# High half first: the streamed weight blocks' sixteen products with the weights' high half ahead of the eight with the low half, each group behind its own wait

## The reference

```python
h = rms_norm(x, norm_g[l]);  proj = h @ w_in[l]            # 1024 x 6728, l = 0, 1
mkv = rms_norm(mem, mem_norm_g[l]) @ w_mem_kv[l]           # 1024 x 1024
merged = g0 * (y_pool @ w_branch[l, 0]) + g1 * (y_attn @ w_branch[l, 1]) + g2 * (y_mem @ w_branch[l, 2])
x = x + merged @ w_out[l]
# second block, 272 tokens
proj = h @ w_in_2                                          # q, k, v, z, b, a, scb, scc, scx, gates
qkv = silu(depthwise_conv_centred(q | k | v, conv_w))      # five taps
h_res = h_res + merged @ w_out_2
h_res = h_res + (silu(gate) * up) @ w_down_2               # D_FF = 2816
```

## Time and profile before

| | |
|---|---|
| median of 3 runs | 1518.5 us |
| the profiled execution: span from first to last instruction | 1512.8 us |
| PE busy (matmuls) | 1356.0 us, 90% |
| PE weight loads busy | 1288.6 us, 85% |
| DVE busy | 860.9 us, 57% |
| ACT busy | 671.8 us, 44% |
| POOL busy | 265.1 us, 18% |

### The profile page before, as it was taken

The page is one execution under the profiler, slowest core; times in us unless marked ns, Lnnn a source line. Parts: engine busy times, 40 slices in busy tenths (PEclk is TensorE's granted clock), DMA queues, the critical chain, the costliest instruction groups (busy, mean ns, idle before and its releaser), DMA issues.

```text
span 1512.8 us, 32274 instructions
## 1 busy us (share of the span) xinstructions
PE 1356.0 (90%) x12138; PEld 1288.6 (85%) x12138; DVE 860.9 (57%) x1352; ACT 671.8 (44%) x1067; POOL 265.1 (18%) x259
## 2 busy tenths in 40 slices
PE   4889989979899989899658799999999899799997
PEld 4878978979799978898548789989989899799997
DVE  4334745546436645555488866666657565555544
ACT  5334435433434445433434553333333453566633
POOL 0000040006000220152042225336235000000000
PEclk9999989989999989999788999999999999999999
DMA  4524543334444523344223332231221454355553
GB/s 184 189 90 154 180 153 112 111 103 161 135 139 142 192 97 125 104 161 140 96 84 107 116 112 79 77 98 59 94 80 61 150 177 144 120 175 172 174 189 110
DMA packets 55481, 194.71 MB, mean 129 GB/s; under 512 B 6248, under 2 KB 9832, under 8 KB 54640
## 3 DMA queue, kind: packets, MB, share of 16 engines
q1 hardware_dynamic: 49248, 179.33, 36.1%
q10 hardware_dynamic: 5856, 13.30, 2.5%
q0 software_dynamic: 304, 1.07, 0.2%
HBM read 189.26 MB, written 4.41 MB: 128 GB/s over the span
## 4 chain that ended last, share of the span: by engine, by line
PE 61%; issue 22%; DVE 8%; ACT 3%; DVEq 2%; POOL 1%; POOLq 1%; DMA 1%; ACTq 0%
PE stream_ps L277 16%; PE stream_ps L279 15%; PE stream_ps L278 15%; DVE w_lo L269 2%; DVE qkvT L1099 2%; PE free_ps L1655 1%; PE free_ps L1638 1%; ACT w_hi L263 1%; PE free_ps L355 1%; PE free_ps L1656 1%; DVEq L1105 1%; POOLq L407 1%; PE free_ps L1403 1%; DMA cst<-cst_dram 1%; DVE oT L362 1%
## 5 line engine op out<-in xcount | busy, mean ns | idle before, releaser
L277 PE MATMUL stream_ps<-h_hi,w_hi 128*128 128x256 f32 (+1 forms) x2016 | 603.0, 299 | 54.8 <-DVE w_lo L269 25.6
L269 DVE TENSOR_TENSOR w_lo<-raw,w_hi 128x1024 fp32r<-128x1024 f32 x342 | 431.4, 1268 | 347.9 <-ACT w_hi L263 341.6
L279 PE MATMUL stream_ps<-h_hi,w_lo 128*128 128x256 f32 (+1 forms) x2016 | 585.6, 290 | 0.0
L278 PE MATMUL stream_ps<-h_lo,w_hi 128*128 128x256 f32 (+1 forms) x2016 | 585.5, 290 | 0.0
L277 PEld LDWEIGHTS stream_ps<-h_hi,w_hi 128*128 128x128 f32 x2016 | 393.4, 195 | 66.2 <-issue 31.9
L278 PEld LDWEIGHTS stream_ps<-h_lo,w_hi 128*128 128x128 f32 x2016 | 392.8, 195 | 0.7 <-issue 0.5
L279 PEld LDWEIGHTS stream_ps<-h_hi,w_lo 128*128 128x128 f32 x2016 | 392.7, 195 | 0.0
L263 ACT ACTIVATE w_hi<-raw 128x1024 fp32r<-128x1024 f32 x342 | 358.6, 1054 | 61.8 <-PE stream_ps L279 55.3
L1222 DVE TENSOR_TENSOR xy<-xy,free_ps 64x128 f32<-64x128 f32 x180 | 44.7, 283 | 62.7 <-PE free_ps L1656 47.4
L1099 DVE SCALAR_TENSOR_TENSOR qkvT<-st_raw,gains,qkvT 128x272 f32<-128x272 f32 x96 | 65.8, 726 | 5.3 <-ACT qkvT L681 2.6
L794 ACT ACTIVATE n<-free_ps 64x128 f32<-64x128 f32 x80 | 22.0, 275 | 105.2 <-PE free_ps L1638 104.3
(11 more groups left out here) (327 smaller groups left out, 2141.6 us busy)
## 6 DMA issues: line engine op xcount, KB each, us to landing
raw<-stream_dram SPq DMA_DIRECT2D x342, 512.0 KB, 3.5
gate_spill<-gate_out ACTq DMA_DIRECT2D x16, 136.0 KB, 2.0
xT<-xT_dram ACTq DMA_DIRECT2D x1, 1088.0 KB, 8.8
stage<-wik_dram ACTq DMA_DIRECT2D x2, 544.0 KB, 4.9
x_spill<-xT ACTq DMA_DIRECT2D x1, 1088.0 KB, 4.0
gb<-gate_spill ACTq DMA_DIRECT2D x1, 1088.0 KB, 7.0
ga<-gate_spill ACTq DMA_DIRECT2D x1, 1088.0 KB, 9.2
xT<-x_spill ACTq DMA_DIRECT2D x1, 1088.0 KB, 5.7
```

The source lines that it names most:

```text
L269: nc.vector.tensor_tensor(w_lo[s][:, :, :], raw[:, s, :].rearrange("p (k n) -> p k n", k=KT), w_hi[s][:, :, :].bitcast(F32), ALU.subtract) ...
L277: nc.tensor.matmul(ps, l_hi, r_hi, start=first, stop=False)
L278: nc.tensor.matmul(ps, l_hi, r_lo, start=False, stop=False)
L279: return nc.tensor.matmul(ps, l_lo, r_hi, start=False, stop=last)
```

## The change

Every streamed block outside `unit` and `gate` now runs in two parts. PE waits for `hi_ready` of the block, makes the sixteen products with the high half of the weights (high x high and high x low of each tile), then waits for `lo_ready`, and makes the eight products low x high. The number of products, their operands and the place of `blk_done` (after the last product) stay. `first_blocks` makes the sixteen products of both of its blocks first (8, 8, 8, 8), then the eight of block 0 and the eight of block 1. In `block_rows` the high products of the first 128 tokens come before the wait, everything else behind it. The steps of the delta rule, and ACT's, DVE's, POOL's and SP's programs, are not touched. One wait is added to each block.

```diff
+        def with_hi(ps, l_hi, r_hi, r_lo, first):
+            nc.tensor.matmul(ps, l_hi, r_hi, start=first, stop=False)
+            nc.tensor.matmul(ps, l_hi, r_lo, start=False, stop=False)
+
         def block_cols(pe, G, s, free, free_at, r_hi, r_lo, parts=None):
-            pe.wait_ge(lo_ready, 4 * G + s + 1 + SLOTS)
+            pe.wait_ge(hi_ready, 4 * G + s + 1)
             pe.wait_ge(free, free_at)
-            n = r_hi.shape[-1]
+            ps = stream_ps[s][:, 0:r_hi.shape[-1]]
             for k in range(KT):
                 if parts and k % 4 == 0:
                     pe.wait_ge(parts[0], parts[1] + k // 4)
-                mm = mm3(stream_ps[s][:, 0:n], w_hi[s][:, k, :], w_lo[s][:, k, :], r_hi[:, k, :], r_lo[:, k, :],
-                         k == 0, k == KT - 1)
+                with_hi(ps, w_hi[s][:, k, :], r_hi[:, k, :], r_lo[:, k, :], k == 0)
+            pe.wait_ge(lo_ready, 4 * G + s + 1 + SLOTS)
+            for k in range(KT):
+                mm = nc.tensor.matmul(ps, w_lo[s][:, k, :], r_hi[:, k, :], start=False, stop=k == KT - 1)
             mm.then_inc(blk_done, 1)

         def first_blocks(pe, G, free, free_at, r_hi, r_lo, parts):
             for half in range(2):
                 for s in range(AHEAD):
                     if half == 0:
-                        pe.wait_ge(lo_ready, 4 * G + s + 1 + SLOTS)
+                        pe.wait_ge(hi_ready, 4 * G + s + 1)
                         pe.wait_ge(free, free_at + s)
                     if s == 0:
                         pe.wait_ge(parts[0], parts[1] + half)
                     for k in range(4 * half, 4 * half + 4):
-                        mm = mm3(stream_ps[s][:, 0:n], w_hi[s][:, k, :], w_lo[s][:, k, :], r_hi[:, k, :], r_lo[:, k, :],
-                                 k == 0, k == KT - 1)
-                    if half:
-                        mm.then_inc(blk_done, 1)
+                        with_hi(stream_ps[s][:, 0:n], w_hi[s][:, k, :], r_hi[:, k, :], r_lo[:, k, :], k == 0)
+            for s in range(AHEAD):
+                pe.wait_ge(lo_ready, 4 * G + s + 1 + SLOTS)
+                for k in range(KT):
+                    mm = nc.tensor.matmul(stream_ps[s][:, 0:n], w_lo[s][:, k, :], r_hi[:, k, :], start=False, stop=k == KT - 1)
+                mm.then_inc(blk_done, 1)

         def block_rows(pe, G, s, free, free_at, l_hi, l_lo):
-            pe.wait_ge(lo_ready, 4 * G + s + 2 + SLOTS)
+            pe.wait_ge(hi_ready, 4 * G + s + 2)
             pe.wait_ge(free, free_at + 1)
             for t in range(2):
...
                 for k in range(KT):
+                    nc.tensor.matmul(ps, l_hi[:, k, toks], w_hi_all[:, s:s + 2, k, :], start=k == 0, stop=False)
+                    nc.tensor.matmul(ps, l_lo[:, k, toks], w_hi_all[:, s:s + 2, k, :], start=False, stop=False)
+                if t == 0:
+                    pe.wait_ge(lo_ready, 4 * G + s + 2 + SLOTS)
+                for k in range(KT):
+                    mm = nc.tensor.matmul(ps, l_hi[:, k, toks], w_lo_all[:, s:s + 2, k, :], start=False, stop=k == KT - 1)
             mm.then_inc(blk_done, 2)
```

More of the change, by code:

```diff
@@ L305, in first_blocks @@
                     for k in range(4 * half, 4 * half + 4):
-                        mm = mm3(stream_ps[s][:, 0:n], w_hi[s][:, k, :], w_lo[s][:, k, :], r_hi[:, k, :], r_lo[:, k, :],
-                                 k == 0, k == KT - 1)
-                    if half:
-                        mm.then_inc(blk_done, 1)
+                        with_hi(stream_ps[s][:, 0:n], w_hi[s][:, k, :], r_hi[:, k, :], r_lo[:, k, :], k == 0)
[4 more added lines that the diff above has]
+                mm.then_inc(blk_done, 1)
         def block_rows(pe, G, s, free, free_at, l_hi, l_lo):
-            pe.wait_ge(lo_ready, 4 * G + s + 2 + SLOTS)
+            pe.wait_ge(hi_ready, 4 * G + s + 2)
             pe.wait_ge(free, free_at + 1)
             for t in range(2):
+                toks = slice(t * P, (t + 1) * P)
+                ps = stream_ps[s][:, t * S:(t + 1) * S].rearrange("p (j n) -> p j n", j=2)
                 for k in range(KT):
-                    tok = slice(t * P, (t + 1) * P)
-                    mm = mm3(stream_ps[s][:, t * S:(t + 1) * S].rearrange("p (j n) -> p j n", j=2), l_hi[:, k, tok], l_lo[:, k, tok],
-                             w_hi_all[:, s:s + 2, k, :], w_lo_all[:, s:s + 2, k, :], k == 0, k == KT - 1)
+                    nc.tensor.matmul(ps, l_hi[:, k, toks], w_hi_all[:, s:s + 2, k, :], start=k == 0, stop=False)
[4 more added lines that the diff above has]
+                    mm = nc.tensor.matmul(ps, l_hi[:, k, toks], w_lo_all[:, s:s + 2, k, :], start=False, stop=k == KT - 1)
             mm.then_inc(blk_done, 2)
@@ L1461, in _ @@
                     for s in range(SLOTS):
-                        pe.wait_ge(lo_ready, 4 * (G + 15 + br) + s + 1 + SLOTS)
+                        pe.wait_ge(hi_ready, 4 * (G + 15 + br) + s + 1)
                         pe.wait_ge(dve_evac, DVE_EVACS * l + 4 * br + s + 1)
+                        y = lambda part, k: part[:, bass.ds(br, 1), k, :].rearrange("p a n -> p (a n)")
                         for c in range(2):
+                            ps = stream_ps[s][:, c * S:(c + 1) * S]
                             for k in range(4):
[L1466 to L1469, removed]
+                                with_hi(ps, w_hi[s][:, 4 * c + k, :], y(y_hi, k), y(y_lo, k), k == 0)
+                            if c == 0:
+                                pe.wait_ge(lo_ready, 4 * (G + 15 + br) + s + 1 + SLOTS)
+                            for k in range(4):
+                                mm = nc.tensor.matmul(ps, w_lo[s][:, 4 * c + k, :], y(y_hi, k), start=False, stop=k == 3)
                         mm.then_inc(blk_done, 1)
@@ L1718, in _ @@
                     c, s = n // 3, n % SLOTS
-                    pe.wait_ge(lo_ready, 4 * G_DOWN + 12 * w + n + 1 + SLOTS)
+                    pe.wait_ge(hi_ready, 4 * G_DOWN + 12 * w + n + 1)
                     if n % 3 == 0:
                         pe.wait_ge(dve_evac, D2 + 84 + 4 * w + c + 1)
[L1722 to L1725, removed]
+                    kfs = range(KT * (n % 3), min(FT, KT * (n % 3) + KT))
+                    for k, kf in enumerate(kfs):
+                        with_hi(stream_ps[c][:, 0:T], w_hi[s][:, k, :], f_hi[:, kf, :], f_lo[:, kf, :], kf == 0)
+                    pe.wait_ge(lo_ready, 4 * G_DOWN + 12 * w + n + 1 + SLOTS)
+                    for k, kf in enumerate(kfs):
+                        mm = nc.tensor.matmul(stream_ps[c][:, 0:T], w_lo[s][:, k, :], f_hi[:, kf, :], start=False, stop=kf == FT - 1)
                     mm.then_inc(blk_done, 1)
```

## The result

The changed kernel takes 1524.9 us (median of 11 runs, 1521.5 to 1528.9) beside 1517.7 for the kernel before on the same chip: ratio 1.0055, 95% interval 1.0036 to 1.0074. It is slower by 0.55%, where 1.1% faster was forecast. The profiled execution has a span of 1526.9 us, 14.1 more than before.

The account below looks back on a forecast made before the run. PE was taken as the bound (61% of the chain, plus 22% its issue time). Terms -0.4 - 5.0 - 4.3 - 8.5 + 1.5 = -16.7 us took 1518.5 to 1501.8, with 50% on 1498 to 1505.5; range 1497 to 1512.

Parts of the forecast that it names:

- the added wait: zero: One more wait in each of 292 blocks costs nothing; 24 products across a block border still take 2.84 us.
- slower: Rival, 6%: the wait inside each block lets the array run dry, 0.1 us for 292 blocks, 29 us: 1531.
- Step 1: Four second pairs of `block_rows`: PE starts after the high half alone, 1.26 us earlier each, minus 5.0 us.
- Block 2: PE stands 0.26 us before its low half, plus a longer first product; gain taken as 0.4 us.
- Step 2: Behind three row-pair waits the clock stays at 2.4 GHz instead of falling to 1.2, 1.43 us each: minus 4.3 us.
- the clock does not come back: Rival, 14%: the three row-pair places give no clock gain, up to 1.4 us more lost: about -11.4, 1507.1.
- Step 3: q, k, v stage: high products run in PE's idle time, so handovers to DVE come earlier: minus 8.5 us.
- only the first handover: Rival, 20%: DVE as the bound eats the q, k, v stage's later gains, leaving 2.1 us: -10.3, 1508.2.
- the sums near 846: Sign for the q, k, v stage: sums at 863.29 move earlier by 8.5 and the 8.8 us gained before.
- POOL's product: q, k, v stage: the 5.92 us product falls on block 197's low half instead of a tap, paid once.
- Step 4: `first_blocks` signals block 0 after 40 products, not 36; four products paid in three w_out stages, plus 1.5 us overall.
- The output projections: PE gains 1.26 us at 1225.98, but idle time at 1232.99 grows from 0.73 to 2.0 us: gain zero.

Follow-up runs that it names:

- the row pairs alone: New order only in the 16 row pairs, against the kernel before, steps loop at its old place: 1511.5 us, ratio 0.9967.
- both parts: New order in the row pairs and the q, k, v stage, against the kernel before, steps loop at its old place: 1505.2 us, ratio 0.9920.
- the padded one: Changed kernel plus 436 already met waits (218 instructions) at PE's start, bringing the steps loop to its old offset: 1523.3 us, ratio 1.0033.
- shared values: Changed kernel with the high halves' semaphore started at 4, so both waits compare one value and the loop keeps its old place: 1505.6 us, ratio 0.9923.
- the stage alone: New order only in 22 blocks of the q, k, v stage, against the kernel before, steps loop at its old place: 1515.3 us, ratio 0.9995.
- without the first groups: Full new order with the steps loop in place, but `first_blocks` groups of w_out, q, k, v stage and gate-up in old order: 1508.2 us, ratio 0.9933.
- the first groups alone: Kernel before with only the `first_blocks` groups of w_out, q, k, v stage and gate-up in new order, loop in place: 1522.0 us, ratio 1.0023.

## Why the prediction was wrong

**Its sum left out the term that decided.** Steps 1 to 4 made -16.7 us. With the loop in place the change gives -11.7 (1518.15 x 0.0077); the move of the loop adds 19.3 us (1524.9 against 1505.6; 21.2 in the trace), and the forecast had no step for it. The step that failed is the fifth, "the added wait: zero". It asked what a wait costs on PE's queue and what is queued behind it, and there it was right: 2.84 us from block to block, as in the earlier trace rows:

```profile
179.74 0.28 PE L283 MATMUL stream_ps<-h_hi,w_hi 128*128 128x256 f32 x1
...
182.58 0.28 PE L283 MATMUL stream_ps<-h_hi,w_hi 128*128 128x256 f32 x1
```

It didn't ask what instructions the wait brings along, nor what length does to PE's largest loop. The rival "slower" had the sign and nearly the time (1531), but by another mechanism (an array that runs dry in each block), and that one measured zero.

**Step 1, row pairs, -5.0: right.** PE starts 0.05 us behind the high half, with 1.4 to 1.5 us idle in place of 2.7; the first products of the four pairs start 1.26 us earlier each, measured against the matmul ahead of them, 5.0 in all. Block 2 gained 0.5 (0.4 forecast).

```profile
46.97 0.38 PE L329 MATMUL stream_ps<-w_hi,mem_hi 128*128 128x256 f32 x1 [1.42 <-ACT w_hi L263]
...
71.20 0.38 PE L329 MATMUL stream_ps<-w_hi,mem_hi 128*128 128x256 f32 x1 [1.42 <-ACT w_hi L263]
...
463.02 0.38 PE L329 MATMUL stream_ps<-w_hi,h_hi 128*128 128x256 f32 x1 [1.49 <-ACT w_hi L263]
```

**Step 2, the clock, -4.3: right at its three places, zero in the changed kernel's sum.** Behind each pair the granted clock is 1.00 where it was 0.50 to 0.55, and the distance grows there by 1.6, 1.3 and 1.5 us, 4.4:

```profile
71.30:74.30 3.00, 3.00 (x26) 3.00 (x27) 2.33 (x2) 1.08 (x2) 0.00 (x0) 1.00 0.18 44
...
148.60:151.40 2.80, 2.80 (x25) 2.80 (x26) 2.71 (x4) 1.69 (x4) 0.00 (x0) 1.00 0.23 41
463.20:466.00 2.80, 2.80 (x25) 2.80 (x25) 2.71 (x4) 1.68 (x4) 0.00 (x0) 1.00 0.14 22
```

But it fell elsewhere. The matmuls of layer 0's first blocks ran at 0.50 in the changed kernel and at 1.00 before:

```profile
100.00:103.00 3.00, 3.00 (x15) 3.00 (x16) 0.00 (x0) 0.00 (x0) 0.00 (x0) 0.50 0.00 0
```
```profile
104.00:106.00 2.00, 2.00 (x18) 2.00 (x19) 0.00 (x0) 0.00 (x0) 0.00 (x0) 1.00 0.00 0
```

That took 4.1 us back (-4.6 at 95.35 to -0.5 at 107.08). It needn't have: with the row pairs alone, and with both parts (the table's last column), layer 0's first blocks kept the high level. Outside the steps loop 455 matmuls started at the low clock after the change, 453 before it. So of the two cases that the forecast weighed, the rival "the clock does not come back" gives the better sum (-12.4 without its extra 1 us, against the -11.7 measured), for a reason that it didn't name: the clock comes back where the wait was, and goes elsewhere. As step 3 in both sums is uncertain by more than they differ, that is a hint and no proof. Which matmuls the clock takes differs from kernel to kernel where neither work nor order does; the runs don't show what decides it.

**Step 3, the q, k, v stage, -8.5: right in its inside, its size known only to some 3 us.** From 726 to 869 the gain on the trace of the kernel before is 8.7 us in the changed kernel, 6.9 in the padded one, 7.0 with shared values, 9.4 with the stage alone, 9.3 with both parts and 7.8 without the first groups, 8.2 in the mean. But kernels that have the old order there gain on it too: 3.0 to 3.1 us the five that only add padding or waits, 0.1 with the row pairs and 0.5 with the first groups alone, 2.3 in the mean. The trace of the kernel before has 113 low matmuls in this stretch, those five 80 or 81. Against this mean the step is worth 5.9 us: clearly more than the 2.1 of the rival (only the first handover), and perhaps less than 8.5. The inside went as told: block 182's sixteen high products ran ahead of its wait, whose length stayed 11.19 us; the first taps start at 784.16, 2.8 us earlier once the 1.9 us with which the stage was entered are taken off (2.1 forecast), the second at 815.21, 5.6 us earlier (4.7), and the sums at 852.63, 8.8 earlier (8.5). The forecast had looked for the sums near 846; the stage was entered 1.9 us early, not the 8.8 that it had counted, for the two reasons given below the table and in step 2.

```profile
776.81 0.59 PE L298 MATMUL stream_ps<-h_hi,w_lo 128*128 128x272 f32 x1 [11.19 <-DVE w_lo L269]
...
784.16 3.88 DVE L1113 SCALAR_TENSOR_TENSOR qkvT<-st_raw,gains,qkvT 128x272 f32<-128x272 f32 x8 [0.21 <-ACT qkvT L695]
...
815.21 3.87 DVE L1113 SCALAR_TENSOR_TENSOR qkvT<-st_raw,gains,qkvT 128x272 f32<-128x272 f32 x8
...
836.73 9.32 DVE L1113 SCALAR_TENSOR_TENSOR qkvT<-st_raw,gains,qkvT 128x272 f32<-128x272 f32 x8
847.24 2.18 PE L298 MATMUL stream_ps<-h_hi,w_lo 128*128 128x272 f32 x8 [5.21 <-DVE w_lo L269]
...
852.63 0.39 PE L1540 MATMUL free_ps<-wide,cst 128*128 128x272 f32 x1
```

One detail was wrong without an effect: POOL's product fell on a tap again (9.32 us for eight, as in the earlier trace rows), not on a low half. As forecast, it was paid once. By the rule of the Trainium skill, "TensorE: Matmul & The Clock Gate", the part on oscillation, that waits between bursts of matmuls send the clock down again and again, waits inside a block might have eaten this gain. The trace agrees that the clock is low behind such a wait: the granted clock was 0.50 from 776.90 to 781.50, as from 779.40 to 784.60 before the change. It was no lower or longer than before, and the gain stood.

**Step 4, costs, +1.5: right in kind.** In layer 0's w_out the first addition waits 2.21 us in place of 1.68 and the last square follows 22.6 us later, as before, so the four products are paid in full, 0.5 us:

```profile
379.00 0.43 DVE L1066 TENSOR_TENSOR xT<-stream_ps,xT 128x256 f32 x1 [2.21 <-PE stream_ps L317]
...
401.60 0.42 ACT L659 ACTIVATE wide<-xT  x1 [1.75 <-DVE xT L1066]
```

Layer 1 shows 0.5 (2.20 in place of 1.70 us idle before its first addition) and the second block, in the kernel with shared values, 0.5 too (3.16 in place of 2.68); in the changed kernel 14 low matmuls ahead of it make it 4.54. That the three places cost 1.5 us of the total was not shown: the two runs meant for it contradict each other, by more than that. The output projections did as forecast: PE gains 1.26 us at 1225.98 and gives it back at 1232.99, where its idle time grows from 0.73 to 1.99 us.

## What to carry to other kernels

Before an edit to an engine's program, count the instructions that it adds and look which loops are near the size that stays resident: here a loop of 1773 instructions stays, by the count of pieces, only from 20 of 256 offsets, and in one place twelve instructions more in front of it cost 18 us. The sign in the profile is idle time put down to "issue" at the first instruction behind a jump back, with instruction packets in the queues' view of one pass. Where two waits can compare with the same value, let them (start the semaphore at the offset): the shared value gave this change its gain back, 1505.6 us against 1524.9. And take no gain for the clock from single places: it came back at all three, and the sum over the changed kernel stayed. Nor take the size of a step from one pair of traces: kernels with the old order in the q, k, v stage differed there by 3 us.

## What was not expected of the hardware

- Eight pieces of 16 KB of PE's instructions stay, the one fetched ahead counted, as the four places of this loop have it. When it needed nine it fetched all nine in every pass, and each jump back cost 4.2 to 4.6 us of idle PE, with 1.5 to 2.7 us more for the clock behind it.
- A wait on a matmul that is already met costs nothing measurable in 292 blocks. A wait that stands as an instruction of its own takes about 0.11 us on PE's queue (218 of them 24 us, 13.5 beyond the 10.5 us of idle time that covered the rest).
- The number of matmuls outside the steps loop that ran at the low clock went from 425 to 513 over the traces of fourteen kernels with nearly the same work, at some 0.1 us each; many of these stretches follow no wait of PE (60 of them in the last pass of the loop with the row pairs alone). An edit worth 1 or 2 us could not be read from the total time here; it has to be read at its place in the trace, and the same place in other kernels tells how far that can be trusted.
